# The opening stage of a hybrid encoder step: past gates summed earlier, a fourth modulation buffer, the first norm tile by tile

## The chip, the cores and the metric

One core of one Trainium2 chip runs the whole program. The metric is the device time of one execution in microseconds, as the median of several runs.

## The reference

One layer of a streaming encoder works on T = 1152 tokens: 1024 of one new stream (the prompt) and 8 x 16 of running streams (the samples), each of 1024 channels, all in float32.

```python
def rms_norm(x, g):
    inv = lax.rsqrt(jnp.mean(xf * xf, axis=-1, keepdims=True) + EPS)
    return (xf * inv).astype(x.dtype) * g

def ffn_sublayer(x, mod, base, g, w1, w3, w2):
    h = modulate(rms_norm(x, g), mod[:, base], mod[:, base + 1])   # h * (1 + scale) + shift
    gate = 1 + mod[:, base + 2][:, None, :]
    return x + MACARON_W * gate * swiglu(h, w1, w3, w2)
```

`mod` is silu(c) @ w_ada + b_ada, nine vectors of 1024 for each of the nine sequences. The layer is: this feed-forward, a mixer (a recurrent branch and a forgetting attention), a second feed-forward, and a final norm with a modulation of its own. The attention of the samples needs the running sum of `cache_logf`, the log forget gates of 1024 past positions for 8 streams and 16 heads (the **past gates**).

## The kernel before

**Layout.** Activations lie transposed: `x` is [128 channels, 8 channel tiles k, 1152 tokens], cut into three chunks c of 384 tokens (the third holds 256 of the prompt and all 128 of the samples). Every product is made of three passes (`mm3`, L299, L302, L303): an activation is split into a high part (`acts_hi`, by ScalarE) and the rest (`acts_lo`, by VectorE), a weight block of [128, 2048] into `w_hi` (ScalarE, L283) and `w_lo` (GpSimd, L289). A feed-forward goes over 11 pairs of 256 hidden channels; a pair is six `up` units (unit n is chunk n // 2, half n % 2, 48 matmuls each), then three `down` parts. In the first nine pairs of the first feed-forward a quarter of the rest of the modulation follows each of the first units (`ada_step`: TensorE makes a product, VectorE copies it to `mod_part`, TensorE turns it, VectorE adds the bias).

**Who sets the order.** Each engine runs a program written out by hand, and semaphores tie them; nothing is scheduled by a planner. What stands behind a waiting instruction on its engine waits too. All loads go through SyncE's queue in the order in which they are issued.

**The opening stage, by engine.** SyncE (`setup_sync`) loads the conditioning rows, the nine row tiles of x, small vectors, three slices of `w_ada` (slices 0 to 2, 2 MB each), the first two weight blocks, and, after the first slice was used (`ada_full`), slice 3 into the buffer of slice 0, the state rows, the forget columns `wfl_raw`, and the past gates, as eight loads whose pieces are 16 floats.
TensorE (`setup_tensor`) turns c and x, sums the squares for each chunk (`norm_sum_all`, L670, eight matmuls with a matrix of ones), and makes the first modulation: `product(h)` (L482) and `turn(h)` (L489) for four slices h, in the order product 0, product 1, turn 0, product 2, turn 1, turn 2, product 3, turn 3. Then `setup_rest_tensor` turns states and past gates (L551 to L558) and waits until both running sums are done (`past_summed` 3). Only then does `ffn_tensor` begin.
ScalarE (`setup_scalar`) squares x (L664), takes three roots (L676), makes three constants (L435 to L439), and goes on with `ffn_blocks_ahead` (the high parts of the first two weight blocks), the first norm, and `setup_rest_scalar` (an Exp and a Ln, each behind a table load, for the decay of the recurrence, and `wfl_hi`).
VectorE (`setup_vector`) moves x out of PSUM (L591), and for each chunk takes the reciprocal (L680) and multiplies the whole chunk by it (L685); then it copies the modulation rows (`copy_rows`, L601), adds biases (L565), and makes the scale (`final_scale`, L571, which releases the semaphore `mod_final`).

**The first norm.** Chunks 0 and 1 are made ahead of the feed-forward, chunk by chunk: VectorE modulates five of eight channel tiles (L707), ScalarE three (L718); ScalarE copies the chunk as a whole to `acts_hi` (L726), VectorE subtracts as a whole for `acts_lo` (L731) and releases `h_lo`, on which `up` waits. After chunk 1 VectorE runs `setup_rest_vector`: the rest of the decay (`log1p_vector`, `wfl_lo`), the states and the two running sums (L336). Chunk 2 is made behind unit 1. The later norms are made tile by tile with other helpers: `scale_tiles` (L815, x times scale times reciprocal, which is read in PSUM), `hi_tiles` (L844), `lo_tiles` (L860).

## Time and profile before

| | us |
|---|---|
| median of 3 runs | 3422.22 |
| lowest and highest | 3420.77, 3422.83 |
| the profiled execution | 3419.37 |
| its span in the trace | 3416.4 |

The profile is of one execution. Times in it run from the start of its span; the execution's own time is 2.97 us more than the span. A group of instructions is named by line, engine, operation and tile; "idle before" is the time in which its engine had nothing to do ahead of it, with what ended that time. PE is TensorE, PEld its weight loads, DVE VectorE, ACT ScalarE, POOL GpSimd, SP SyncE.

### The profile page before, as it was taken

How to read it: one execution, taken by the hardware profiler on the slowest of the kernel's cores; microseconds unless marked ns; L12 is line 12 of the kernel's file. 1: busy time of each engine (PE TensorE's matmuls, PEld its weight loads, DVE VectorE, ACT ScalarE, POOL GpSimd, SP SyncE). 2: the span in 40 equal slices, each digit the busy share in tenths (PEclk: the TensorE clock that was granted, in tenths of full speed). 3: DMA queues.
4: the chain of work that ended last, by engine and by line, in shares of the span. 5: the costliest groups of instructions: out<-in, count | busy, mean ns of one | idle time of the engine just before them, and what ended most of it. 6: DMA issues, size and time to landing. Idle time of an engine off the chain costs nothing.

```text
span 3416.4 us, 53101 instructions
## 1 busy us (share of the span) xinstructions
PE 3268.3 (96%) x20609; PEld 3113.7 (91%) x20609; DVE 1267.4 (37%) x2560; ACT 987.2 (29%) x1564; POOL 910.5 (27%) x471
## 2 busy tenths in 40 slices
PE   5999999999998999999999998889999999999997
PEld 3999999999988999998877797889989999999997
DVE  6322222222267342452222216775444222233225
ACT  3111111111143233333333416883232111111114
POOL 1222222222241211111110124773233222232223
PEclk7999999999999999999999999999999999999999
DMA  6322232231121321217777755664311111111101
GB/s 207 99 86 86 91 103 88 89 96 62 38 82 35 105 85 63 97 51 243 245 239 261 250 166 125 144 143 150 130 38 62 37 37 37 37 49 37 47 27 56
DMA packets 254331, 352.01 MB, mean 103 GB/s; under 512 B 40189, under 2 KB 190261, under 8 KB 253938
## 3 DMA queue, kind: packets, MB, share of 16 engines
q1 hardware_dynamic: 227762, 316.87, 29.4%
q10 hardware_dynamic: 26432, 33.18, 2.7%
q8 instruction: 103, 1.69, 0.2%
q14 instruction: 34, 0.28, 0.0%
HBM read 297.74 MB, written 48.07 MB: 101 GB/s over the span
## 4 chain that ended last, share of the span: by engine, by line
PE 87%; DVE 6%; issue 3%; ACT 3%; POOL 1%; DMA 0%; ACTq 0%; SPq 0%; DVEq 0%; POOLq 0%
PE psum L299 25%; PE psum L303 25%; PE psum L302 25%; PE psum L1779 2%; PE psum L2253 2%; PE psum L2272 1%; PE psum L482 1%; PE psum L1826 1%; DVE w_lo L2461 1%; PE psum L1420 1%; PE psum L1793 1%; PE psum L2238 1%; DVE acts_lo L860 1%; PE psum L489 1%; PE psum L2239 1%
## 5 line engine op out<-in xcount | busy, mean ns | idle before, releaser
L299 PE MATMUL psum<-acts_hi,w_hi 128*128 128x384 f32 x4032 | 1394.3, 346 | 26.8 <-DVE past_rows L336 25.2
L302 PE MATMUL psum<-acts_lo,w_hi 128*128 128x384 f32 x4032 | 1358.6, 337 | 6.0 <-issue 6.0
L303 PE MATMUL psum<-acts_hi,w_lo 128*128 128x384 f32 x4032 | 1358.8, 337 | 0.0
L299 PEld LDWEIGHTS psum<-acts_hi,w_hi 128*128 128x128 f32 x4032 | 761.5, 189 | 64.7 <-issue 47.5
L289 POOL TENSOR_TENSOR w_lo<-w_raw,w_hi 128x2048 fp32r<-128x2048 f32 x106 | 489.4, 4624 | 1175.1 <-ACT w_hi L283 1175.1
L303 PEld LDWEIGHTS psum<-acts_hi,w_lo 128*128 128x128 f32 x4032 | 760.7, 189 | 6.3 <-issue 6.3
L302 PEld LDWEIGHTS psum<-acts_lo,w_hi 128*128 128x128 f32 x4032 | 762.0, 189 | 4.4 <-issue 0.9
L1143 DVE TENSOR_TENSOR u_f<-psum,gated 128x384 f32<-128x384 f32 x132 | 73.6, 558 | 1020.2 <-ACT gated L1039 1020.2
L1094 POOL TENSOR_TENSOR u_lo<-u_f,u_hi 128x384 fp32r<-128x384 f32 x132 | 134.7, 1020 | 937.4 <-ACT u_hi L1044 937.4
L1214 DVE SCALAR_TENSOR_TENSOR x<-psum,mods,x 128x384 f32<-128x384 f32 (+1 forms) x552 | 314.5, 570 | 183.7 <-PE psum L303 183.7
L283 ACT ACTIVATE w_hi<-w_raw 128x2048 fp32r<-128x2048 f32 x106 | 200.4, 1909 | 572.0 <-PE psum L299 536.8
L299 PE MATMUL psum<-u_hi,w_hi 128*128 128x384 f32 x1056 | 356.4, 337 | 3.4 <-DVE x L1219 2.2
L303 PE MATMUL psum<-u_hi,w_lo 128*128 128x384 f32 x1056 | 355.6, 337 | 0.0
L302 PE MATMUL psum<-u_lo,w_hi 128*128 128x384 f32 x1056 | 355.5, 337 | 0.0
L1039 ACT ACTIVATE gated<-psum 128x384 f32<-128x384 f32 x132 | 64.8, 491 | 889.9 <-PE psum L303 889.8
L299 PEld LDWEIGHTS psum<-u_hi,w_hi 128*128 128x128 f32 x1056 | 199.0, 188 | 4.9 <-DVE x L1219 3.3
L302 PEld LDWEIGHTS psum<-u_lo,w_hi 128*128 128x128 f32 x1056 | 199.0, 188 | 0.3
L303 PEld LDWEIGHTS psum<-u_hi,w_lo 128*128 128x128 f32 x1056 | 199.1, 189 | 0.0
L1993 DVE COPY kTs<-psum 128x512 f32<-128x512 f32 x64 | 44.3, 692 | 249.8 <-PE psum L1779 249.8
L2253 PE MATMUL psum<-ident,pr 128*128 128x128 f32 x576 | 92.9, 285 | 31.9 <-DVE w_lo L2461 27.9
L2461 DVE TENSOR_TENSOR w_lo<-psum,w_hi 128x512 fp32r<-128x512 f32 (+1 forms) x192 | 100.4, 551 | 27.4 <-ACT w_hi L2338 26.7
L2253 PEld LDWEIGHTS psum<-ident,pr 128*128 128x128 f32 x576 | 63.4, 142 | 46.7 <-DVE w_lo L2461 29.9
(267 smaller groups left out, 2974.0 us busy)
## 6 DMA issues: line engine op xcount, KB each, us to landing
w_raw<-in_ffn_w SPq DMA_DIRECT2D x66, 1024.0 KB, 5.3
kc<-in_cache_k SPq DMA_DIRECT2D x32, 1024.0 KB, 6.7
vc<-in_cache_v SPq DMA_DIRECT2D x16, 2048.0 KB, 7.8
w_raw<-in_w_ada SPq DMA_DIRECT2D x28, 1024.0 KB, 5.0
w_raw<-in_w_in SPq DMA_DIRECT2D x28, 1024.0 KB, 5.3
sp<-sample_bias SPq DMA_DIRECT2D x128, 65.0 KB, 2.5
ada_w<-in_w_ada SPq DMA_DIRECT2D x4, 2048.0 KB, 15.1
w_raw<-in_w_ada_f SPq DMA_DIRECT2D x8, 1024.0 KB, 5.6
```

What stands on the lines that cost most here:

```text
L283: eng.activation(w_hi[st][:], w_raw[raw][:], ACT.Copy).then_inc(sem("w_hi_done"), 1)
L289: eng.tensor_tensor(w_lo[st][:], w_raw[raw][:], w_hi[st][:].bitcast(F32), ALU.subtract).then_inc(sem("w_lo_done"), 1)
L299: pass1 = eng.matmul(out, whi, ahi, start=first, stop=False)
L302: eng.matmul(out, whi, alo, start=False, stop=False)
L303: return eng.matmul(out, wlo, ahi, start=False, stop=last)
L1039: eng.activation(gated[n % 2][:], ps[2 * (n % 2)][:, 0:CH], ACT.Silu).then_inc(sem("gated_ready"), 1)
L1094: eng.tensor_tensor(u_lo[:, t, tokens_of(c)], u_f[n % 2][:], u_hi[:, t, tokens_of(c)].bitcast(F32), ALU.subtract).then_inc(sem("u_lo_done" ...
L1143: eng.tensor_tensor(u_f[n % 2][:], ps[2 * (n % 2) + 1][:, 0:CH], gated[n % 2][:], ALU.mult).then_inc(sem("u_free"), 1)
L1214: last = eng.scalar_tensor_tensor(xt[:, d, t0:t0 + cp], bank[:, 0:cp], mods[:, gate, d, 0:1], xt[:, d, t0:t0 + cp], ALU.mult, ALU.add)
L1779: last = eng.transpose(ps[TURNED][:, 128 * m:128 * m + 128], kc[:, 4 * half + m, 128 * p:128 * p + 128], ident[:])
L2253: last = eng.transpose(ps[bank_of(k, n)][:, 128 * (kb - k0):128 * (kb - k0) + 128], pr[k % 4][:, 128 * kb:128 * kb + 128], ident[:])
L2461: eng.tensor_tensor(pT_lo[q % 2][:, k0:k1, cols_], ps[bank_of(k, n)][:, 0:128 * (k1 - k0)].rearrange("p (k n) -> p k n", n=128), pT_hi[q % ...
```

## The change

The past gates and the states are loaded right behind x, the past gates in one load whose pieces are 128 floats, into `past_in`; GpSimd reorders them into `past_rows`; TensorE turns them between the sums of squares of chunk 0 and chunk 1 (half of the partitions at a time, with j, the position within a partition, as the innermost step of the result), and VectorE sums them (`past_sums`) behind the first reciprocal. `setup_rest_scalar` moves ahead of the first weight split, `setup_rest_vector` ahead of the first `copy_rows`. The fourth slice of `w_ada` gets `ada_w3`, over the rows of x, and is loaded ahead of the first weight blocks. `turn(1)` goes ahead of `product(2)`. The first norm uses the later norms' helpers; the whole multiply L685 goes, the samples' modulation moves to GpSimd, and the order on ScalarE is weight block 0, chunk 0, weight block 1, chunk 1. TensorE's first pair leaves the loop and is written out, and its first unit waits for weight block 1 only ahead of the second half of its products.

```diff
@@ -76,6 +76,9 @@
     xrowf = ExitStack()
     x_rows = [sb(xrowf, f"x_rows{n}", [128, D]) for n in range(T // 128)]
     xrowf.close()
+    adaf = ExitStack()
+    ada_w3 = sb(adaf, "ada_w3", [128, KT, 512])
+    adaf.close()
@@ -118,6 +121,7 @@
     adaf.close()
+    ada_w.append(ada_w3)
@@ -136,6 +140,7 @@
     past_rows = sb(setup, "past_rows", [128, PAST // 128, SB * H])
+    past_in = sb(setup, "past_in", [128, SB, PAST // 128, H])
@@ -378,21 +383,19 @@
-        def load_half(h, slot):
-            eng.dma_start(ada_w[slot][:], w_ada_v[:, :, 512 * h:512 * h + 512]).then_inc(sem(f"ada_loaded{slot}"), 16)
-        for h in range(3):
-            load_half(h, h)
-        ffn1_loads_ahead(eng)
-        eng.wait_ge(sem("ada_full"), 1)
-        load_half(3, 0)
+        eng.dma_start(past_in[:].rearrange("p b j h -> p b (j h)"),
+                      a["cache_logf"][0].rearrange("b (p j) h -> p b (j h)", p=128)).then_inc(sem("past_loaded"), 16)
         eng.dma_start(state_rows[0][:], a["state_rglru"].rearrange("l s (r c) -> (l s r) c", c=128)).then_inc(sem("state_loaded"), 16)
         conv_src = a["state_conv"].rearrange("l s j (r c) -> (l s j r) c", c=128)
         for n in range(2):
             eng.dma_start(state_rows[1 + n][:], conv_src[96 * n:96 * n + 96, :]).then_inc(sem("state_loaded"), 16)
-        eng.dma_start(wfl_raw[:], kview(a["w_in"][0])[:, :, COL_FL:COL_FL + H]).then_inc(sem("fl_loaded"), 16)
-        eng.dma_start(b_fgt_col[:], a["b_fgt"].rearrange("l h -> h l")).then_inc(sem("fl_loaded"), 16)
-        for b in range(SB):
-            eng.dma_start(past_rows[:, :, H * b:H * b + H], a["cache_logf"][0, b].rearrange("(k p) h -> p k h", p=128)).then_inc(sem("past_loaded"), 16)
+        for h in range(4):
+            if h == 3:
+                eng.wait_ge(sem("x_turned"), 2 * 4 + CREDIT)
+                eng.dma_start(wfl_raw[:], kview(a["w_in"][0])[:, :, COL_FL:COL_FL + H]).then_inc(sem("fl_loaded"), 16)
+                eng.dma_start(b_fgt_col[:], a["b_fgt"].rearrange("l h -> h l")).then_inc(sem("fl_loaded"), 16)
+            eng.dma_start(ada_w[h][:], w_ada_v[:, :, 512 * h:512 * h + 512]).then_inc(sem(f"ada_loaded{h}"), 16)
+        ffn1_loads_ahead(eng)
@@ -437,6 +440,7 @@
         eng.activation(pick_r[:], mask_f[0:ST, :], ACT.Copy).then_inc(sem("const_split"), 1)
+        setup_rest_scalar(eng)
@@ -468,6 +472,9 @@
                           pattern=[[-1, 128]], channel_multiplier=1).then_inc(sem("const"), 1)
+        eng.wait_ge(sem("past_loaded"), 16)
+        eng.tensor_copy(past_rows[:].rearrange("p j (b h) -> p j b h", b=SB),
+                        past_in[:].rearrange("p b j h -> p j b h")).then_inc(sem("past_loaded"), 1)
         eng.wait_ge(sem("const_split"), 2)
@@ -490,7 +497,7 @@
-    START_BANKS = (5, 3)
+    START_BANKS = (7, 3)
@@ -519,14 +526,17 @@
         eng.wait_ge(sem("params_ready"), 1)
-        for c in range(NC):
-            norm_sum_all(eng, 0, c)
+        eng.wait_ge(sem("x_moved"), 2 * (T // 128) + CREDIT)
+        norm_sum_all(eng, 0, 0)
+        setup_rest_tensor(eng)
+        norm_sum_all(eng, 0, 1)
+        norm_sum_all(eng, 0, 2)
 
         def product(h):
-            eng.wait_ge(sem(f"ada_loaded{h % 3}"), 16 * (h // 3 + 1))
+            eng.wait_ge(sem(f"ada_loaded{h}"), 16)
             if h >= 2:
                 eng.wait_ge(sem("mod_rows_ready"), h - 1)
-            ada_product(eng, ps[START_BANKS[h % 2]], ada_w[h % 3], 512)
+            ada_product(eng, ps[START_BANKS[h % 2]], ada_w[h], 512)
 
         def turn(h):
...
         eng.wait_ge(sem("c_act"), 2)
-        eng.wait_ge(sem("x_moved"), 2 * (T // 128) + CREDIT)
+        eng.wait_ge(sem("past_summed"), 1)
         product(0)
         product(1)
         turn(0)
+        turn(1)
         product(2)
-        turn(1)
         turn(2)
         product(3)
         turn(3)
@@ -548,16 +558,17 @@
     def setup_rest_tensor(eng):
 
         eng.wait_ge(sem("state_loaded"), 48)
-        eng.transpose(ps[0][:, 0:64], state_rows[0][:], ident[0:64, 0:64])
+        eng.transpose(ps[7][:, 0:64], state_rows[0][:], ident[0:64, 0:64])
         for n in range(2):
-            last = eng.transpose(ps[0][:, 64 + 96 * n:160 + 96 * n], state_rows[1 + n][:], ident[0:96, 0:96])
+            last = eng.transpose(ps[7][:, 64 + 96 * n:160 + 96 * n], state_rows[1 + n][:], ident[0:96, 0:96])
         last.then_inc(sem("states_turned"), 1)
-        eng.wait_ge(sem("past_loaded"), 16 * SB)
+        eng.wait_ge(sem("past_loaded"), 17)
         for half in range(2):
-            for k in range(4):
-                last = eng.transpose(ps[1 + half][:, 128 * k:128 * k + 128], past_rows[:, 4 * half + k, :], ident[:])
+            rows = slice(64 * half, 64 * half + 64)
+            for j in range(PAST // 128):
+                last = eng.transpose(ps[1 + half].rearrange("q (p j) -> q p j", j=PAST // 128)[:, :, j],
+                                     past_rows[rows, j, :], ident[rows, rows])
             last.then_inc(sem("states_turned"), 1)
-        eng.wait_ge(sem("past_summed"), 3)
@@ -590,9 +601,11 @@
-        for c in range(NC):
-            norm_inverse(eng, 0, c)
-            norm_times_inverse(eng, 0, c)
+        norm_inverse(eng, 0, 0)
+        past_sums(eng)
+        norm_inverse(eng, 0, 1)
+        norm_inverse(eng, 0, 2)
+        setup_rest_vector(eng)
@@ -624,18 +637,20 @@
         eng.tensor_tensor(wfl_lo[:], wfl_raw[:], wfl_hi[:].bitcast(F32), ALU.subtract).then_inc(sem("past_summed"), 1)
+        eng.memset(tiny_col[:], 2.0 ** -100)
+
+    def past_sums(eng):
         eng.wait_ge(sem("states_turned"), 1)
-        eng.tensor_copy(h0[:], ps[0][:, 0:64])
-        eng.tensor_copy(conv_state[:], ps[0][:, 64:256])
+        eng.tensor_copy(h0[:], ps[7][:, 0:64])
+        eng.tensor_copy(conv_state[:], ps[7][:, 64:256])
         past_f = past_rows[:].rearrange("p k n -> p (k n)")
         for half in range(2):
             eng.wait_ge(sem("states_turned"), 3)
             if half:
-                eng.wait_ge(sem("past_summed"), 2)
+                eng.wait_ge(sem("past_summed"), 1)
             running_sums(eng, past_f[:, 512 * half:512 * half + 512], ps[1 + half], past_f[:, 511:512] if half else 0.0).then_inc(sem("past_summed"), 1)
-        eng.wait_ge(sem("past_summed"), 3)
+        eng.wait_ge(sem("past_summed"), 2)
         eng.tensor_copy(past_last[:], past_rows[:, PAST // 128 - 1, 127:128])
...
 
-    STAT_BANKS = [(6, 7, 4), (7, 2, 5), (6, 7, 6), (7, 2, 7)]
+    STAT_BANKS = [(0, 5, 6), (7, 2, 5), (6, 7, 6), (7, 2, 7)]
@@ -679,67 +694,22 @@
-    def norm_times_inverse(eng, n, c):
-
...
-    def norm_scale(eng, n, c):
-
...
-    def norm_hi(eng, n, c):
-
...
-    def norm_lo(eng, n, c):
-
...
     def norm_scalar(eng):
-        for c in range(2):
-            norm_hi(eng, 0, c)
+        eng.wait_ge(sem("ada_full"), FIRST - 1)
+        ffn_split_hi(eng, 0, 0, 0)
+        hi_tiles(eng, 0, 0)
+        ffn_split_hi(eng, 0, 0, 1)
+        hi_tiles(eng, 0, 1)
 
     def norm_vector(eng):
-        for c in range(2):
-            norm_scale(eng, 0, c)
-            norm_lo(eng, 0, c)
+        scale_tiles(eng, 0, 0)
+        lo_tiles(eng, 0, 0)
+        scale_tiles(eng, 0, 1)
+        lo_tiles(eng, 0, 1)
+        samples_inverse(eng, 0)
@@ -756,13 +726,13 @@
     def normed_count(n, c, k):
-        return NC + (n - 1) * NC * KT + c * KT + k + 1
+        return n * NC * KT + c * KT + k + 1
 
     def tile_count(n, c, k):
-        return NC + (n - 1) * (NC * KT + 1) + c * KT + k + 1
+        return n * (NC * KT + 1) + c * KT + k + 1
 
     def sample_count(n, step):
-        return 1 + 3 * (n - 1) + step
+        return 3 * n + step
@@ -954,9 +924,11 @@
             if n == 0:
-                wait_block(eng, block0 + i * 3 + 1)
+                wait_block(eng, block0 + i * 3 + (0 if first and f == 0 else 1))
             for which, bank in ((0, 2 * (n % 2)), (1, 2 * (n % 2) + 1)):
                 whi, wlo = wcols(FFN_SLOTS[which][2], t)
+                if first and f == 0 and (n, which) == (0, 1):
+                    wait_block(eng, block0 + i * 3 + 1)
                 for k in range(KT):
@@ -1011,11 +983,10 @@
+        body(0, first=True, ada=f == 0)
         if f == 0:
-            with eng.Fori(0, ADA_PAIRS) as i:
+            with eng.Fori(1, ADA_PAIRS) as i:
                 body(i, ada=True)
-        else:
-            body(0, first=True)
@@ -1043,7 +1014,8 @@
             if f == 0 and first_step and n == 1:
-                norm_hi(eng, 0, 2)
+                hi_tiles(eng, 0, 2)
+                hi_samples(eng, 0)
@@ -1108,6 +1080,7 @@
         if f == 0:
             for j in range(2):
                 split_lo(eng, block0 + j, FFN_SLOTS[j])
+            samples_modulate(eng, 0)
         with eng.Fori(0, FF_PAIRS - 1) as i:
@@ -1154,9 +1127,10 @@
             for n in range(6):
                 unit(i, n)
+                if f == 0 and first_step and n == 0:
+                    scale_tiles(eng, 0, 2)
                 if f == 0 and first_step and n == 1:
-                    norm_scale(eng, 0, 2)
-                    norm_lo(eng, 0, 2)
+                    lo_tiles(eng, 0, 2)
@@ -1361,7 +1335,7 @@
     def proj_tensor(eng):
-        eng.wait_ge(sem("past_summed"), 1)
+        eng.wait_ge(sem("past_summed"), 3)
...
@@ -2694,12 +2668,6 @@
-    def ffn_blocks_ahead(eng):
-        eng.wait_ge(sem("ada_full"), 3)
-        ffn_split_hi(eng, 0, 0, 0)
-        eng.wait_ge(sem("ada_full"), FIRST)
-        ffn_split_hi(eng, 0, 0, 1)
@@ -2717,9 +2685,7 @@
         setup_scalar(eng)
-        ffn_blocks_ahead(eng)
         norm_scalar(eng)
-        setup_rest_scalar(eng)
         ffn_scalar(eng, 0)
@@ -2746,7 +2712,6 @@
         setup_tensor(eng)
-        setup_rest_tensor(eng)
         ffn_tensor(eng, 0)
@@ -2760,7 +2725,6 @@
         setup_vector(eng)
         norm_vector(eng)
-        setup_rest_vector(eng)
         ffn_vector(eng, 0)
```

## Rows read from the trace of the kernel before

**Rows 1.** The page, busy time of TensorE over the span: us (share), instructions.

```profile
PE 3268.3 (96%) x20609; PEld 3113.7 (91%) x20609; DVE 1267.4 (37%) x2560; ACT 987.2 (29%) x1564; POOL 910.5 (27%) x471
```

**Rows 2.** Waits of TensorE, whole span: us in total, times, longest us.

```profile
PE psum L299 <- DVE past_rows L336: 25.2, 1, 25.2
...
PE psum L302 <- issue: 6.0, 2, 3.0
```

**Rows 3.** Timeline of TensorE, opening: start us, us, instructions, [idle before <-releaser].

```profile
19.70 15.65 PE L670 MATMUL psum<-sq,ones 128*128 128x384 f32 x48
...
44.45 1.88 PE L489 MATMUL psum<-cols,mod_rows 128*128 128x9 f32 x8 [5.54 <-DVE mod_rows L601]
46.26 3.64 PE L482 MATMUL psum<-ada_w,states 128*32 128x512 f32 x16
...
56.72 1.25 PE L558 MATMUL psum<-ident,past_rows 128*128 128x128 f32 x8
83.20 0.68 PE L299 MATMUL psum<-acts_hi,w_hi 128*128 128x384 f32 x1 [25.23 <-DVE past_rows L336]
```

**Rows 4.** Timeline of VectorE, opening; L591 moves x, L571 makes the scale.

```profile
15.35 6.06 DVE L591 COPY x<-psum 128x512 f32<-128x512 f32 x10
...
40.44 3.35 DVE L685 TENSOR_TENSOR h_f<-x,psum 128x3072 f32<-128x3072 f32 x1
43.71 1.28 DVE L601 COPY mod_rows<-psum 128x512 f32<-128x512 f32 x2
...
56.63 4.51 DVE L571 SCALAR_TENSOR_TENSOR mods<-mods,params 128x72 f32<-128x72 f32 x1
...
78.51 0.12 DVE L363 TENSOR_TENSOR lam_t<-lam_t 128x8 f32<-128x8 f32 x1
...
79.55 0.28 DVE L626 TENSOR_TENSOR wfl_lo<-wfl_raw,wfl_hi 128x128 fp32r<-128x128 f32 x1
...
80.15 1.21 DVE L336 TENSOR_TENSOR_SCAN past_rows<-ones,psum 128x512 f32<-128x512 f32 x1
...
104.15 0.56 DVE L1143 TENSOR_TENSOR u_f<-psum,gated 128x384 f32<-128x384 f32 x1 [8.59 <-ACT gated L1039]
...
129.66 0.56 DVE L1143 TENSOR_TENSOR u_f<-psum,gated 128x384 f32<-128x384 f32 x1 [10.13 <-ACT gated L1039]
...
139.56 0.56 DVE L1143 TENSOR_TENSOR u_f<-psum,gated 128x384 f32<-128x384 f32 x1 [8.62 <-ACT gated L1039]
```

**Rows 5.** Timeline of ScalarE, opening.

```profile
35.38 0.56 ACT L676 ACTIVATE psum<-psum,cols 128x384 f32<-128x384 f32 x1 [4.61 <-PE psum L670]
...
37.12 0.31 ACT L439 ACTIVATE pick_r<-mask_f 16x128 fp32r<-16x128 f32 x1 [0.76 <-POOL mask_f L474]
...
74.17 0.19 ACT L444 ACTIVATE lam_t<-params 128x8 f32<-128x8 f32 x1
...
75.90 1.28 ACT L346 ACT_TABLE_LOAD   x1
```

**Rows 6.** Timeline of GpSimd, opening: the first two weight blocks' low parts.

```profile
51.96 9.09 POOL L289 TENSOR_TENSOR w_lo<-w_raw,w_hi 128x2048 fp32r<-128x2048 f32 x2 [14.87 <-ACT w_hi L283]
```

**Rows 7.** Timeline of VectorE, later norms, 945 to 1010 us.

```profile
987.43 4.31 DVE L860 SCALAR_TENSOR_TENSOR acts_lo<-h_f,mods,acts_hi 128x384 fp32r<-128x384 f32 x8
```

**Rows 8.** Timeline of VectorE, 2490 to 2585 us.

```profile
2549.45 4.29 DVE L815 SCALAR_TENSOR_TENSOR h_f<-x,mods,psum 128x384 f32<-128x384 f32 x8
```

**Rows 9.** Timeline of GpSimd, 2490 to 2585 us.

```profile
2571.47 4.80 POOL L289 TENSOR_TENSOR w_lo<-w_raw,w_hi 128x2048 fp32r<-128x2048 f32 x1
```

**Rows 10.** Instructions of line L860: ns min/median/max, first and last start us, forms.

```profile
L860 DVE SCALAR_TENSOR_TENSOR acts_lo<-h_f,mods,acts_hi x48: 472/606/4834, 957.0 to 2579.2; 128x384 fp32r<-128x384 f32 x32, 128x256 fp32r<-128x256 f32 x16
```

**Rows 11.** Stage table: stretch, us, busy us (x) by engine, clock, DMA share, GB/s.

```profile
83.20:88.10 4.90, 4.90 (x15) 4.90 (x16) 0.00 (x0) 3.19 (x2) 2.13 (x1) 0.50 0.95 313
```

**Rows 12.** Timeline of SyncE's queue: start us, us to issue, transfers.

```profile
37.26 0.37 SPq L382 DMA_DIRECT2D ada_w<-in_w_ada  x1
```

**Rows 13.** DMA, loads issued 37.6 to 38.2 us: count, KB each, us to landing.

```profile
h_rows<-in_state_rglru SPq DMA_DIRECT2D x1, 32.0 KB, 7.8
```

More of the change, by code:

```diff
@@ L633, in setup_rest_vector @@
             if half:
-                eng.wait_ge(sem("past_summed"), 2)
+                eng.wait_ge(sem("past_summed"), 1)
             running_sums(eng, past_f[:, 512 * half:512 * half + 512], ps[1 + half], past_f[:, 511:512] if half else 0.0).then_inc(sem("past_summed"), 1)
-        eng.wait_ge(sem("past_summed"), 3)
+        eng.wait_ge(sem("past_summed"), 2)
         eng.tensor_copy(past_last[:], past_rows[:, PAST // 128 - 1, 127:128])
-        eng.memset(tiny_col[:], 2.0 ** -100)
     def mods_rest(eng):
@@ L680, in norm_inverse @@
         eng.reciprocal(stats(n, c), stats(n, c)).then_inc(sem("inv_ready"), 1)
-    def norm_times_inverse(eng, n, c):
-        eng.wait_ge(sem("inv_ready"), NC * n + c + 1)
-        eng.tensor_tensor(h_f[:, :, tokens_of(c)], x[:, :, tokens_of(c)],
-                          stats(n, c).unsqueeze(1).to_broadcast([128, KT, CH]), ALU.mult).then_inc(sem("x_normed"), 1)
     def mods_ready(eng, n):
         eng.wait_ge(sem("mod_final"), 1 if n == 0 else 7)
-    def norm_scale(eng, n, c):
-        g = NC * n + c
-        shift, scale = NORM_MODS[n]
-        if n > 0:
-            norm_times_inverse(eng, n, c)
-        mods_ready(eng, n)
-        eng.wait_ge(sem("x_normed"), g + 1)
-        cp = CH if c < NC - 1 else CP
-        if c == NC - 1:
-            hs = h_f[:, :, TP:T].rearrange("p k (s t) -> p k s t", s=SB)
-            eng.tensor_tensor(hs, hs, seq_bc(scale), ALU.mult).then_inc(sem("mod_step"), 1)
-            eng.wait_ge(sem("mod_step"), n + 1)
-            eng.tensor_tensor(hs, hs, seq_bc(shift), ALU.add)
-        for k in range(K_ON_ACT):
-            hp = h_f[:, k, CH * c:CH * c + cp]
-            last = eng.tensor_scalar(hp, hp, mods[:, scale, k, 0:1], mods[:, shift, k, 0:1], ALU.mult, ALU.add)
-        last.then_inc(sem("h_ready"), 1)
@@ L710, in norm_modulate @@
-    def norm_modulate(eng, n, c):
-        cp = CH if c < NC - 1 else CP
-        shift, scale = NORM_MODS[n]
-        mods_ready(eng, n)
-        eng.wait_ge(sem("x_normed"), NC * n + c + 1)
-        for k in range(K_ON_ACT, KT):
-            hp = h_f[:, k, CH * c:CH * c + cp]
-            last = eng.activation(hp, hp, ACT.Identity, scale=mods[:, scale, k, 0:1], bias=mods[:, shift, k, 0:1])
-        last.then_inc(sem("h_modulated"), 1)
-    def norm_hi(eng, n, c):
-        norm_modulate(eng, n, c)
-        eng.wait_ge(sem("h_modulated"), NC * n + c + 1)
-        eng.wait_ge(sem("h_ready"), NC * n + c + 1)
-        eng.activation(acts_hi[:, :, tokens_of(c)], h_f[:, :, tokens_of(c)], ACT.Copy).then_inc(sem("h_hi"), 1)
@@ L728, in norm_lo @@
-    def norm_lo(eng, n, c):
-        eng.wait_ge(sem("h_hi"), NC * n + c + 1)
-        eng.tensor_tensor(acts_lo[:, :, tokens_of(c)], h_f[:, :, tokens_of(c)],
-                          acts_hi[:, :, tokens_of(c)].bitcast(F32), ALU.subtract).then_inc(sem("h_lo"), 1)
-    def norm_scalar(eng):
-        for c in range(2):
-            norm_hi(eng, 0, c)
-    def norm_vector(eng):
-        for c in range(2):
-            norm_scale(eng, 0, c)
-            norm_lo(eng, 0, c)
+    def norm_scalar(eng):
+        eng.wait_ge(sem("ada_full"), FIRST - 1)
[3 more added lines that the diff above has]
+        hi_tiles(eng, 0, 1)
@@ L1245, in turn @@
             else:
-                eng.wait_ge(sem("h_modulated"), NC + c * KT + KT)
+                eng.wait_ge(sem("h_modulated"), c * KT + KT)
             if tile == 1:
```

## The prediction

> **What bounds the kernel now.** The page comes first: TensorE is busy for 96% of the span [rows 1], so time can come back only where it stands still. The list of its waits then names the places. One wait of 25.2 us stands out: the first product of the feed-forward waits for the running sums of the past gates [rows 2]. Its timeline shows the same as a start: TensorE is done with the opening at about 58.0 us (56.72 + 1.25) and begins the feed-forward at 83.20 [rows 3]. The timelines of the other engines, read between those two points, show what was done meanwhile: the scale on VectorE ends at 61.14 (56.63 + 4.51), then chunks 0 and 1 of the norm are made, and only behind both come the sums [rows 4]. A second loss lies inside the first pair: unit 1 is taken up by VectorE at 104.15, unit 3 at 129.66, which is 25.51 us for two units, while units 3 and 4 stand 9.90 us apart [rows 4]. Two units at 9.90 would be 19.80, so 5.7 us are lost there, behind the third chunk's norm. After this pair TensorE runs nearly without waits, so what the opening gains or loses reaches the end whole.
>
> **Part 1: the way to the first copy of modulation rows.** The first sum of squares now waits for all of x, which is there at 21.4 us (15.35 + 6.06), not 19.70: 1.7 us later. The three sums took 15.65 together, 5.22 each [rows 3]. Behind the first stand the turns. The state rows are the old ones, some 0.6 us; the eight turns of past gates took 1.25 us [rows 3] and become sixteen of half the rows. That costs 1.25 us if the columns count and 2.5 if each instruction does; I take 1.9, between them. The third sum then ends at 21.5 + 15.65 + 0.6 + 1.9 = 39.6 us, where the third root started at 35.38 before [rows 5]: 4.3 later. The loads and GpSimd's reordering lie beside this: GpSimd took 9.09 us for two passes over 128x2048 with two inputs [rows 6], so at most 2.3 us for 1024 with one, and the turns need it only at 26.7 us (21.5 + 5.2). If that cover is gone, the wait stands on TensorE (third rival).
>
> ScalarE then does its constants, which end 2.05 us behind the root's start (37.12 + 0.31 - 35.38), and the decay moved here: from 74.17 to 77.18 (75.90 + 1.28), plus one small Ln of about 0.2, is 3.2 us [rows 5]. So the Ln is done at 39.6 + 2.05 + 3.2 = 44.9. VectorE's part behind it ran from 78.51 to 79.83, 1.3 us [rows 4]; its earlier steps lie beside the table load. With 0.1 to hand over, the first copy of rows starts at 46.3 instead of 43.71 [rows 4], **2.6 us later**. The whole multiplies L685 that go (3.35 us each) were what held it at 43.71 [rows 4]; the running sums take their place on VectorE, but while TensorE makes the second sum, so they cost nothing.
>
> **Part 2: from the copy to the scale.** This took 12.92 us (43.71 to 56.63) [rows 4]. The pieces stay; with turn 1 ahead of product 2 the third copy (0.64) and a bias (about 0.2) are no longer beside a turn, so I add 0.8; the ends are 0 and, if TensorE's clock rises earlier and product 2 takes half of its 3.64 us [rows 3], -1.8. That puts the scale at 60.0. It will not run at once. Of the 72 elements it works on, an instruction should take a fraction of a microsecond, yet it lasted 4.51 us and ended at 61.14, just as GpSimd ended its two weight passes, 61.05 (51.96 + 9.09) [rows 4, 6]. So it stood behind GpSimd. In the changed kernel only weight block 0 is split there. GpSimd began 2.06 us after product 2 ended (49.90, 46.26 + 3.64) [rows 3, 6], and product 2 now ends at about 54.6 at the latest (46.3, 0.74 to the turn, two turns of 1.88, 3.64, and 0.2), or 1.8 earlier: the pass of 4.55 us then ends between 59.4 and 61.2. The scale is done at about **61.0, where it was before**; the fourth slice in its own buffer is there long before it is needed, as slice 3 was before, and brings nothing by itself.
>
> **Part 3: from the scale to the first product.** Before: 83.20 - 61.14 = 22.06 us for two chunks, the decay and the sums. Now one chunk by tiles: eight scale tiles took 4.29 us [rows 8] and eight low tiles 4.31 [rows 7] where the later norms run, the high tiles beside them. Handing over is about 0.2. That alone would start TensorE at 61.0 + 8.8 = 69.8.
>
> But the second weight block's split now stands behind chunk 0's high tiles on ScalarE. The last of those ends about 0.6 us (a tile) behind the scale tiles, at 65.9; GpSimd starts 2.06 us later, at 68.0, as above. The low tiles began at 65.3, so five of eight are done (0.54 each) and three are not. One low tile in the trace took 4.834 us against a median of 0.606 [rows 10], where GpSimd made a weight pass of 4.80 us [rows 9]: 4.2 us lost. Scale tiles read the reciprocal in PSUM and have no such outlier that I found, low tiles have both inputs in SBUF. I charge **4.2 us**, with ends 0 and 4.6: the first product at 74.0, 9.2 us earlier than before.
>
> The Trainium skill, Advanced Engine Details and Errata, section VectorE Performance Modes, says that GpSimd and those VectorE instructions that use two ports, the doubled modes, block each other. By that note alone a low tile, float32 with two inputs, would not be held, and the first product would come at 69.8. The skill's SBUF — State Buffer, section SBUF: two separate sides, adds VectorE instructions with two SBUF inputs, and the row of 4.834 us sides with it.
>
> TensorE starts at the lower clock either way: the first 4.9 us behind the old wait ran at a granted clock of 0.50, which is 1.2 of its 2.4 GHz [rows 11], and it stands idle ahead of the first product here too. No change.
>
> **Part 4: the third chunk.** Its scale tiles now follow unit 0 on VectorE, its low tiles unit 1, the samples' modulation is on GpSimd, long done. VectorE takes unit 1 at about 95.0 (104.15 - 9.2), and TensorE needs the next modulation copy behind unit 2, about 9 us later (the spacing of 9.90 less its step), at 104; eight shorter tiles, beside ScalarE's, take at most 4.3, the samples' parts some 2.5, so it is there at about 102. The wait goes: **5.7 us**. The margin is 2 us.
>
> **Part 5: edits with one answer.** Writing out TensorE's first pair issues the same instructions; the second feed-forward is already written so. Unknown is its loading of code: 0 to 6.0 us (the two stops "issue" of 3.0 us each [rows 2] are the nearest); I take 0, as no such stop lies in either feed-forward. The finer wait for weight block 1 costs nothing: it is there at 72.6, before the first product. Semaphore counts and PSUM banks change no work.
>
> **Sum.** -9.2 - 5.7 = -14.9 us. The profiled execution took 3419.37 (span 3416.4 and 2.97 around it), so 3404.5 by its own time; it lies 2.85 us under the median, which gives **3407.3** against 3422.22, or -0.44%. This kernel's measurement can tell about 0.2%, 6.8 us, from no change.
>
> **Rivals.** *No collision on the low tiles.* If GpSimd starts 1.6 us later than I say, or a low tile is not held, by the first of the two rules above, 4.2 us come back: 3403.1. For it: three tiles are a thin margin. Against it: the row of 4.834 us. Chance 0.15.
>
> *A wait takes the old one's place in the first pair.* If VectorE, with twice as many tile instructions to hand to and fro with ScalarE and with GpSimd's low parts of unit 1 in between, gets to the modulation copy after TensorE, the loss of the first pair returns, up to 5.7: 3413.0. It decides from 2 us of delay on. Chance 0.13.
>
> *Slower: the past gates come late.* TensorE's second and third sums now stand behind them. A state load of 32 KB issued behind a slice of 2 MB, itself issued at 37.26 [rows 12], took 7.8 us to land [rows 13], so landing about 45.5. If the early loads shared the queue with all that follows instead of going first, they would land when the queue runs empty, at about 47.5 (45.5 and the past gates' own share), GpSimd would be done at 49.7, and the turns would come 23.0 us behind 26.7: 3430.3. The time is slower by over 0.2% from 21.7 us of that wait on. Against it: that same row shows a queue served in order, and the past gates are issued ahead of the slices. Chance 0.05.
>
> *Smaller gains together*, the wait in the pair and stops for code, 3419 at the most: chance 0.07, within 0.2% of before.
>
> **Chances and range.** My forecast has 0.60, 3404.5 to 3410.5 by the bounds on turns, clock and code. With the first two rivals 0.88 lies within 3402.5 and 3413.5, the range. Faster by over 0.2%: 0.60 + 0.15 + 0.13 = 0.88; same 0.07; slower 0.05.
>
> **What would show it.** Right: the first product at 74 us; one low tile of chunk 0 lasting 4 to 5 us beside GpSimd's second weight pass; the scale done at 61; units 1 to 4 taken up 9.5 to 9.9 us apart. Wrong: a wait of TensorE on the past gates' reordering at 27 us; the first copy of rows later than 48; a low tile series of 4.3 us; a clock of 0.50 in unit 3.

## The result and the profile after

| | before | after |
|---|---|---|
| median, us (lowest to highest, runs) | 3422.52 (3420.77 to 3424.86, 4) | **3399.73** (3396.57 to 3401.43, 4) |
| profiled execution, us (span) | 3419.37 (3416.4) | 3401.43 (3399.6) |

The ratio is 0.9937, with a 95% interval of 0.9925 to 0.9948: faster by 22.8 us, where 14.9 were predicted, and 2.8 us below the range. The two profiled executions differ by less, 16.8 us of span, since that of before lies under its median and that of after over it. All lines of time below are set against these two.

The timeline of TensorE after the change answers to [rows 3]. Some line numbers have moved: L685 sums squares, L489 makes products, L496 and L569 turn, L304 is the first pass of a product.

```profile
21.97 5.40 PE L685 MATMUL psum<-sq,ones 128*128 128x384 f32 x16 [1.64 <-issue]
...
27.81 1.02 PE L569 MATMUL psum<-ident,past_rows 64*128 64x64 f32 x16
28.76 10.59 PE L685 MATMUL psum<-sq,ones 128*128 128x384 f32 x32
...
46.65 1.06 PE L496 MATMUL psum<-cols,mod_rows 128*128 128x9 f32 x8 [3.73 <-DVE mod_rows L614]
48.09 1.85 PE L496 MATMUL psum<-cols,mod_rows 128*128 128x9 f32 x8 [0.38 <-DVE mods L576]
49.87 3.64 PE L489 MATMUL psum<-ada_w,states 128*32 128x512 f32 x16
54.51 1.85 PE L496 MATMUL psum<-cols,mod_rows 128*128 128x9 f32 x8 [1.01 <-DVE mods L576]
56.29 3.64 PE L489 MATMUL psum<-ada_w,states 128*32 128x512 f32 x16
60.75 1.87 PE L496 MATMUL psum<-cols,mod_rows 128*128 128x9 f32 x8 [0.81 <-DVE mod_rows L614]
71.78 0.66 PE L304 MATMUL psum<-acts_hi,w_hi 128*128 128x384 f32 x1 [9.16 <-issue]
...
98.30 1.93 PE L489 MATMUL psum<-w_raw,states 128*32 128x256 f32 x16 [6.57 <-DMA w_raw<-in_w_ada]
```

The feed-forward begins at 71.78 us instead of 83.20, 11.4 earlier. The last row is new: in the first pair TensorE waits 6.57 us for a transfer, the second quarter of the next modulation weights. VectorE's timeline (compare [rows 4]; L614 copies rows, L582 makes the scale, L785 the scale tiles, L830 the low tiles, L795 the samples):

```profile
45.91 0.69 DVE L614 COPY mod_rows<-psum 128x512 f32<-128x512 f32 x1
...
62.89 0.23 DVE L582 SCALAR_TENSOR_TENSOR mods<-mods,params 128x72 f32<-128x72 f32 x1
63.16 4.29 DVE L785 SCALAR_TENSOR_TENSOR h_f<-x,mods,psum 128x384 f32<-128x384 f32 x8
67.36 4.32 DVE L830 SCALAR_TENSOR_TENSOR acts_lo<-h_f,mods,acts_hi 128x384 fp32r<-128x384 f32 x8
71.60 4.29 DVE L785 SCALAR_TENSOR_TENSOR h_f<-x,mods,psum 128x384 f32<-128x384 f32 x8
...
80.19 1.21 DVE L795 TENSOR_TENSOR h_f<-x,psum 128x1024 f32<-128x1024 f32 x1
```

GpSimd's timeline (compare [rows 6]; L294 makes the low part of a weight block, L804 and L806 modulate the samples):

```profile
55.57 4.54 POOL L294 TENSOR_TENSOR w_lo<-w_raw,w_hi 128x2048 fp32r<-128x2048 f32 x1 [14.47 <-ACT w_hi L288]
69.98 6.17 POOL L294 TENSOR_TENSOR w_lo<-w_raw,w_hi 128x2048 fp32r<-128x2048 f32 x1 [9.87 <-ACT w_hi L288]
81.55 1.94 POOL L804 TENSOR_TENSOR h_f<-h_f,mods 128x1024 f32<-128x1024 f32 x1 [5.40 <-DVE h_f L795]
83.57 1.95 POOL L806 TENSOR_TENSOR h_f<-h_f,mods 128x1024 f32<-128x1024 f32 x1
85.47 4.62 POOL L294 TENSOR_TENSOR w_lo<-w_raw,w_hi 128x2048 fp32r<-128x2048 f32 x1
```

And SyncE's queue between 75 and 100 us:

```profile
90.11 0.37 SPq L280 DMA_DIRECT2D w_raw<-in_ffn_w  x1
90.52 0.58 SPq L865 DMA_DIRECT2D w_raw<-in_w_ada  x1
```

Read together, the last three views show the new wait as a chain: VectorE's sample step (80.19), GpSimd's two sample steps, only then its pass over weight block 2 (ends at 90.09), and with that the buffer is free for the next weight block (90.11), behind which the modulation quarter is issued (90.52). ScalarE had the high part of block 2 ready at 78.35, so GpSimd came to its pass 7.1 us late:

```profile
76.44 1.91 ACT L288 ACTIVATE w_hi<-w_raw 128x2048 fp32r<-128x2048 f32 x1
```

Unit 2 is taken up by VectorE at 110.34, 18.4 us behind unit 1 (91.94). At the end of the first pair (its last unit at 138.99 instead of 148.41) 9.4 us are left of the 11.4.

Matching TensorE's instructions of both traces gives the rest. The lead is 9.8 us at 974 us, and still 9.8 within the first pass of the mixer's projection loop (a product at 1250.09 before stands at 1240.32 after). It is 22.4 within the third pass (1450.09 against 1427.67), and 18.5 at the last product (3411.91 against 3393.38). So **12.6 us appeared in the mixer, in a loop that the change doesn't touch**: from the one product to the other TensorE took 200.0 us before and 187.4 after. Below, the way between these two products is called the mixer's stretch. There the trace of before has its two stops "issue" of 3.0 us [rows 2], one soon behind each jump back to the loop's head, and right at the jump a shorter pause, which the list puts down to ScalarE:

```profile
PE psum L1431 <- ACT st L1488: 2.3, 2, 1.1
```

The trace of after has no wait of TensorE between 1240 and 1450 us. The four pauses add up to 8.3 us. Most of the rest lies in the products behind each stop, which ran at the lower clock (1.2 of 2.4 GHz) before it came back; stretch, us, busy us (x) by engine, clock, DMA share, GB/s:

```profile
1288.00:1293.00 5.00, 4.57 (x15) 4.57 (x15) 0.00 (x0) 0.00 (x0) 0.00 (x0) 0.50 0.03 10
1293.00:1300.00 7.00, 7.00 (x44) 6.93 (x43) 0.00 (x0) 1.77 (x4) 0.00 (x0) 1.00 0.10 28
```

The stops come with transfers of the instruction queue. DMA queues between 1240 and 1450 us, packets, MB, share, first of before:

```profile
q8 instruction: 14, 0.23, 0.4%
```

and of after:

```profile
q8 instruction: 2, 0.03, 0.1%
```

Before, the loop's code is fetched anew in each of the two passes in this stretch, 7 packets each; after, it stays.

### The profile page after: what moved, and what is told of

The parts are those of the page before. It is cut to its first block, busy times and chain, and to the rows that moved or that the text cites. A ratio compares the mean times of both kernels' runs of the same rounds, so it can differ in the third digit from the quotient of the medians.

```text
span 3399.6 us, 53111 instructions
## 1 busy us (share of the span) xinstructions
PE 3269.5 (96%) x20617; PEld 3113.2 (92%) x20617; DVE 1260.7 (37%) x2587; ACT 986.6 (29%) x1577; POOL 916.5 (27%) x474
## 4 chain that ended last, share of the span: by engine, by line
PE 86%; DVE 5%; issue 3%; ACT 3%; SPq 1%; DMA 1%; POOL 1%; ACTq 0%; DVEq 0%; POOLq 0%
PE psum L304 25%; PE psum L308 25%; PE psum L307 25%; PE psum L1753 2%; PE psum L2227 1%; PE psum L489 1%; PE psum L2246 1%; PE psum L1800 1%; DVE w_lo L2435 1%; PE psum L1394 1%; PE psum L1767 1%; DVE acts_lo L830 1%; DVE h_f L785 1%; PE psum L496 1%; PE psum L2212 1%
## 5 line engine op out<-in xcount | busy, mean ns | idle before, releaser
L304 PE MATMUL psum<-acts_hi,w_hi 128*128 128x384 f32 x4032 | 1392.9, 345 | 10.8 <-issue 9.2
L304 PEld LDWEIGHTS psum<-acts_hi,w_hi 128*128 128x128 f32 x4032 | 760.4, 189 | 48.4 <-issue 31.2
L294 POOL TENSOR_TENSOR w_lo<-w_raw,w_hi 128x2048 fp32r<-128x2048 f32 x106 | 491.0, 4639 | 1148.1 <-ACT w_hi L288 1148.1
L304 PE MATMUL psum<-u_hi,w_hi 128*128 128x384 f32 x1056 | 356.3, 337 | 3.4 <-DVE x L1193 2.2
L304 PEld LDWEIGHTS psum<-u_hi,w_hi 128*128 128x128 f32 x1056 | 199.0, 188 | 4.9 <-DVE x L1193 3.3
```

The source lines that it names most:

```text
L294: eng.tensor_tensor(w_lo[st][:], w_raw[raw][:], w_hi[st][:].bitcast(F32), ALU.subtract).then_inc(sem("w_lo_done"), 1)
L304: pass1 = eng.matmul(out, whi, ahi, start=first, stop=False)
```

## The experiments

Each ratio is to the kernel before on the same chip (median 3421.49 us for the four runs whose names begin with e, 3420.28 for f1, f2, g and h, 3420.70 for f3 and both i).

### Undoing the written-out pair, and doing it alone

`e1_rolled` is the changed kernel with TensorE's first pair back in its loop, where the finer wait for weight block 1 then stands in every pair; `e2_writtenout` is the kernel before with only that pair written out. Of the first, the loop:

```diff
...
-        body(0, first=True, ada=f == 0)
         if f == 0:
-            with eng.Fori(1, ADA_PAIRS) as i:
+            with eng.Fori(0, ADA_PAIRS) as i:
                 body(i, ada=True)
+        else:
+            body(0, first=True)
```

> The changed kernel, but TensorE's first pair is back in the loop of nine pairs (the finer wait on weight block 1 is kept, in every pair). Theory (code): writing the pair out moved TensorE's later code, and by that the mixer's projection loop stopped being loaded anew in each pass; back in the loop, two stops 'issue' of 3.0 us with a low clock behind them return near 1280 and 1420 us, the instruction queue moves some 103 packets instead of 90, and the time is about 12 us over the changed kernel's 3399.7, at 3412. The opening and the first pair stay as they are (first product at 71.8). Rival: the mixer gained because everything came earlier and the loads fell otherwise; then the time stays at 3399.7 within 2 us, without stops.

Measured: 3414.69 us, ratio 0.9982 (0.9972 to 0.9991). The opening is that of the changed kernel (first product at 72.50), and the stops are back, longer than before: each now holds the whole pause at its jump. The mixer's stretch takes 202.2 us. Waits of TensorE:

```profile
PE psum L1406 <- issue: 11.0, 2, 5.6
```

> The kernel before, with one edit alone: TensorE's first pair of the first feed-forward is written out ahead of a loop of eight. Theory (code): the two stops in the mixer go although nothing else is changed, about -12.4 us: 3410, first product still at 83.2. Rival: the stops are not of the code's place: 3422.5 as before, with the stops.

Measured: 3422.82 us, ratio 1.0005 (0.9995 to 1.0014), 14 packets, two stops, the longer 3.9 us, and 201.9 us for the stretch. My theory that writing out the pair removes the stops fell: it takes the pair and the other edits together. What they alter in common for the projection loop is how many instructions of TensorE stand ahead of it. Hence the next theory: the loop's *place*.

### The place alone

`f1_before_shifted` and `f3_before_17` are the kernel before with 45 and 17 more instructions at the head of TensorE's program; `f2_after_shifted` is the changed kernel with 200. They are waits for something that is already there (two waits make one instruction).

```diff
         eng.sem_inc(sem("pa_s"), 16)
+        for _ in range(90):
+            eng.wait_ge(sem("w_used"), 1)
         eng.wait_ge(sem("const"), CONSTS)
```

> The kernel before, with 45 more instructions at the head of TensorE's program (waits on a semaphore that already stands, in the first 4 us in which TensorE idles); nothing else differs, and no arithmetic is added. Theory (the place of the mixer's projection loop in TensorE's code decides whether it is fetched again in every pass): with the code ahead of it 45 instructions longer the loop stays loaded; the two stops without a semaphore in the mixer go, the instruction queue moves 1 or 2 packets between 1240 and 1450 instead of 14, and the median is about 14 us lower, 3408 (3404 to 3413). Rival (the stops went because of something else that the change does in the opening): 14 packets, both stops, 3422.

Measured: **3408.35 us**, ratio 0.9965 (0.9952 to 0.9977), 2 packets, no stop in the mixer. The first product stands at 83.47, as before. So 11.9 us of the median came from 45 instructions that do nothing. The mixer's stretch takes 187.4 us, as in the changed kernel: 12.6 gained. To the end 3.9 of that go again, in steps near 1750, 2550 and 3385 us, and the changed kernel loses 3.9 behind the mixer too; what takes them was not tested.

> The kernel before with 17 more instructions at the head of TensorE's program. By the place theory the projection loop is still fetched in every pass (it stays loaded only from about 25 more on), and its first instructions lie closer to the end of their fetched piece than before, as in the run with the rolled pair: stops of about 5 us instead of 3.0 at the two jumps back, 14 or 15 packets, median 3422 to 3427. If the length of the stops has nothing to do with the place: stops of 3.0.

Measured: 3424.67 us, ratio 1.0009 (1.0000 to 1.0019), 14 packets, and both stops longer, as expected; they hold the whole pause at the jump, which before was 1.1 + 3.0. Waits of TensorE:

```profile
PE psum L1433 <- issue: 10.7, 2, 5.4
```

> The changed kernel, with 200 more instructions at the head of TensorE's program (the same kind of wait, in stretches in which TensorE idles for loads). Theory of the place: the loop lies badly again; the stops return, 14 packets between 1240 and 1450, about 15 us more, 3414 (3410 to 3420), and the opening up to the first product within 1 us of the changed kernel's 71.8. Rival: no stops, 3400, or only what the waits themselves cost in the opening.

Measured: 3415.62 us, ratio 0.9982 (0.9973 to 0.9992): the number expected, but not its reason. Waits of TensorE:

```profile
PE psum L513 <- issue: 14.3, 1, 14.3
...
PE psum L307 <- issue: 0.9, 2, 0.5
```

The 200 instructions cost 12 us in the opening (first product at 83.72), which I had taken for nothing. The loop is indeed fetched again (15 packets), but the stops are 0.5 us each, behind pauses of up to 1.2 at the jump, and the mixer's stretch takes 191.5 us, 4.1 more than in the changed kernel. So a fetch need not cost as much.

The stops at this jump had 0.5, 3.0, 3.9, 5.4 and 5.6 us, and the traces show one pattern in them. In all ten jumps with a fetch (before, `e1`, `e2`, `f2`, `f3`) TensorE is past its stop 5.7 to 6.0 us behind the last product of the pass. What differs is how many products and turns it makes in that time: none in `f3` and `e1`, 2 in `e2`, 7 in the kernel before, 22 in `f2`. The 17 instructions of `f3` moved the stop from behind 7 products and turns, each with its weight load, to the loop's head. This fits code that arrives piece by piece, with an edge between two pieces that the place sets; where the edges lie was not measured. The data traffic doesn't tell the cases apart: over the 6 us behind the jump the mean DMA share was 0.64 before, 0.61 in `f2`, 0.52 in `f3` and 0.60 in `f1`, which didn't stop.

### The new wait in the first pair

`e3_unit1_early`: SyncE issues the second modulation quarter ahead of the weight block whose buffer is late.

```diff
             unit(i, 0, view[:, :, ds(col, 256)])
+            if first:
+                unit(i, 1, view[:, :, ds(col + 256, 256)])
             ffn_load(eng, 0, i + 1, 0)
-            for u in range(1, 4):
+            for u in range(2 if first else 1, 4):
```

> The changed kernel, but SyncE issues the second quarter of the modulation's weights in the first pair ahead of the first weight block of the next pair. Theory: the 6.6 us wait of TensorE behind unit 1 is a load that stood in SyncE's queue behind a wait on GpSimd's third weight pass (90.1 us); issued at about 83 it lands at 88, units 1 and 2 are taken up 9.9 us apart instead of 18.4, and the time falls by about 8.5 us to 3391. Rival: VectorE's copy or the samples' part is late as well, then another wait stands in the same place: a gain under 3 us, 3397 or more.

Measured: 3389.98 us, ratio 0.9909 (0.9892 to 0.9925). The wait is gone; timeline of TensorE:

```profile
92.40 1.07 PE L489 MATMUL psum<-w_raw,states 128*32 128x256 f32 x16
...
102.30 1.07 PE L489 MATMUL psum<-w_raw,states 128*32 128x256 f32 x16
```

The modulation products behind units 0 to 2 now stand 9.9 us apart (the first at 82.52). The end of the chain read above is shown by this: the transfer was late by its place in SyncE's queue, not by the traffic. That the samples' steps are what holds the block ahead of it is read from the views; no run moved them.

### The order of the turns

`e4_turn_order`: product 2 ahead of turn 1 again, as before.

```diff
         turn(0)
+        product(2)
         turn(1)
-        product(2)
         turn(2)
```

> The changed kernel, with product 2 ahead of turn 1 again, as before the change. Theory: the new order leaves TensorE standing about 1 us behind each step, its clock stays at 0.50 through products 2 and 3 and turns 1 to 3, and the way from the first copy of rows to the scale takes 17.0 us instead of 12.9; with the old order product 3 takes 1.9 us again instead of 3.6, the scale is made about 4 us earlier (58.7), and the time falls by about 4 us to 3395.7. Rival: the order is free or better as changed, since the clock stays low in either case: 3399.7 to 3401.

Measured: 3394.37 us, ratio 0.9925 (0.9909 to 0.9942), first product at 67.55. The interval overlaps that of the change, and part of the 4.2 us by which this first product leads 71.78 is TensorE's clock. That shows in executions of one order at two clocks. `e2_writtenout`, with the old order, has the opening of the kernel before, and its timeline of TensorE reads:

```profile
44.37 1.87 PE L489 MATMUL psum<-cols,mod_rows 128*128 128x9 f32 x8 [5.53 <-DVE mod_rows L601]
...
58.24 1.88 PE L489 MATMUL psum<-cols,mod_rows 128*128 128x9 f32 x8 [0.81 <-DVE mod_rows L601]
```

From the first to the end of the last turn this is 15.75 us. In the profiled execution of before the same instructions took 11.92 (44.45 to 56.37). From 51.6 on a turn took 1.03 to 1.06 us and a product 1.92, not 1.85 and 3.64: the granted clock was 1.00 from 51.6 to 56.4 us, and 0.50 in `e2_writtenout` from 51.6 to 60.1 (2.4 and 1.2 GHz). `e4_turn_order` itself took 12.05 us (46.34 to 58.39), with the clock up for a part. The new order took 16.78 us at the low clock in `e3_unit1_early` (46.33 to 63.11), and 13.11 in `h_split_early` below (46.34 to 59.45), where the clock rose. So the new order costs 1.0 to 1.2 us, and the moment at which the clock rises is worth 3.7 to 3.8 in either order. What sets that moment stays open: `i_after_again` and three others of the new order stayed at the low clock from 48 us to the last turn, three had it rise between 53 and 70 us; in two of these the edit takes effect only later.

> The changed kernel once more, beside the others of this job: median 3397 to 3402; the second modulation quarter again about 6.5 us late in the first pair. If the opening's clock comes up at another moment of the opening in each execution, the first product lies anywhere from 68 to 73 us in its profile; if the new order of the turns fixes it, at 71.8 within 0.5.

Measured: 3397.82 us, ratio 0.9934 (0.9916 to 0.9952), first product at 71.68, the quarter late by 6.6 us.

`g_both` is `e3_unit1_early` and `e4_turn_order` together.

> The changed kernel with both single edits together: SyncE issues the second modulation quarter ahead of the next weight block in the first pair, and TensorE computes product 2 ahead of turn 1 again. If the two stalls are independent the gains add: 3399.7 - 9.7 - 5.3 = 3384.7 (3382 to 3388). Rival (the opening's gain is taken back by a wait for the same transfers in the first pair): 3390.

Measured: **3387.55 us**, ratio 0.9901 (0.9882 to 0.9920), the lowest median of all: first product at 68.69, units 9.9 us apart. It lies in the range, 2.9 us short of the sum that I gave. Set against `e3_unit1_early` it is 2.4 us lower, within both intervals; the order's own 1.0 to 1.2 would fit as well.

### Who waits, GpSimd or VectorE

`h_split_early` splits weight block 1 on ScalarE ahead of chunk 0's high tiles; `i_split_mid` does it behind the first of them (the diff is of this one).

```diff
-        hi_tiles(eng, 0, 0)
+        hi_tile(eng, 0, 0, 0)
         ffn_split_hi(eng, 0, 0, 1)
+        for k in range(1, KT):
+            hi_tile(eng, 0, 0, k)
```

> The changed kernel, but ScalarE splits weight block 1 ahead of chunk 0's high tiles, so that GpSimd's pass over block 1 (4.6 to 6.2 us) falls beside VectorE's scale tiles or low tiles of chunk 0 instead of behind them. Theory of my prediction (a long GpSimd pass holds a VectorE operation with two SBUF inputs for its whole length): one VectorE tile of 3 to 5 us in the trace, the first product 3 to 4 us later than 71.8, the median 3402 to 3404. Rival (in a row of VectorE operations without a gap GpSimd is the one that waits, as its 6.17 us pass at 69.98 seems to show): all low tiles of chunk 0 stay near 0.53 us, the first product stays within 1 us of 71.8, the median 3398 to 3401.

Measured: 3403.54 us, ratio 0.9950 (0.9932 to 0.9968). This told nothing of the low tiles: GpSimd's second pass ran beside the scale tiles, which took their usual 4.29 us, and ended at 64.78, as the low tiles began at 64.61. That the median lies where the theory put it is no support: the trace has no long tile, its first product stands at 69.03, and it is that of the fastest of the four executions (3396.90). What makes the others 6 to 8 us longer stays open.

> The changed kernel, but ScalarE splits weight block 1 right behind chunk 0's first high tile, so that GpSimd's pass over it starts about 66.3, while VectorE still writes the scale tiles, and is under way when the low tiles begin at 67.4. Theory (whoever begins first keeps the other waiting: a pass of GpSimd that is under way holds a VectorE operation with two SBUF inputs to its end; a closed row of such VectorE operations holds GpSimd): the first low tile takes 3.5 to 4 us instead of 0.53, the first product comes 3.4 us later, at 75 to 76, and the median 3 us above the changed kernel of the same job. Rival (low tiles are not held by GpSimd in this place, whatever begins first): all low tiles near 0.53 us, first product 71 to 73, no difference.

Measured: 3400.18 us, ratio 0.9944 (0.9926 to 0.9963), 2.4 above `i_after_again`, within both intervals. In the trace the collision happens. GpSimd, then VectorE (the series that took 4.32):

```profile
63.65 4.52 POOL L294 TENSOR_TENSOR w_lo<-w_raw,w_hi 128x2048 fp32r<-128x2048 f32 x1 [3.33 <-ACT w_hi L288]
...
64.65 7.63 DVE L832 SCALAR_TENSOR_TENSOR acts_lo<-h_f,mods,acts_hi 128x384 fp32r<-128x384 f32 x8
```

The same line by duration, ns min/median/max:

```profile
L832 DVE SCALAR_TENSOR_TENSOR acts_lo<-h_f,mods,acts_hi x8: 607/609/3928, 64.7 to 71.7; 128x384 fp32r<-128x384 f32 x8
```

One tile took 3.93 us, from its start to the end of GpSimd's pass and a tile more. The first product came at 72.39, 3.4 us behind the 69.03 of `h_split_early`, whose clock rose alike.

## Why the prediction was wrong, step by step

By the profiled executions the terms are: first product -11.4 us (predicted -9.2), first pair +2.0 (predicted -5.7), mixer and what follows it -12.6 + 3.9 = -8.7 (predicted 0). With 0.4 us gained between pair and mixer and 1.7 lost behind the last product that is -16.8, the difference of the spans. Two misses of 7.7 and 8.7 us with opposite signs nearly cancel, so that the forecast came as near as it did is luck. The medians differ by 6.0 us more: the profiled execution of before lies 3.15 us under its median, that of after 1.70 over, and 1.1 lies outside the spans.

**Part 5 failed, "I take 0, as no such stop lies in either feed-forward."** It asked whether the written-out pair would bring stops of its own where it stands. The runs show that added instructions move the code behind them, and that the mixer's loop was the one to gain: 12.6 us in the change and in `f1_before_shifted` alike, 3.9 given back later in both. The row that carried my bound of 6.0 us [rows 2] was the thing itself. I read it as a price, and did not ask what two stops without a semaphore, at the jump of one loop, come from. My bounds also had the wrong sign: code could only cost. The Trainium skill, Advanced Engine Details and Errata, section ISA Cache, gives TensorE 128 KB for instructions in lines of 16 KB, 256 instructions. An estimate from that page: the loop's pass has 780 products and turns and 65 other instructions in the trace; with a weight load for each of the 780, as the page of the profile counts them, that is 1625, or 6.35 lines, which lie across seven or eight lines by place, out of eight. The 7 packets a pass, of 16 KB each (0.23 MB in 14), agree; that eight lines are what fails is not shown.

**Part 4 failed, "the samples' modulation is on GpSimd, long done".** The old wait went, but the samples' steps stand ahead of weight block 2 in GpSimd's program, and SyncE's queue waits for that block. I followed VectorE to the modulation copy and did not follow the moved step on the engine that received it, with what is queued behind it there. `e3_unit1_early` removes the new wait of 6.6 us. My second rival had the right place and the wrong engine: it asked for a delay on VectorE.

**Part 3, the charge of 4.2 us, did not fall due.** The eight low tiles took 4.32 us, none over 0.62 in chunk 0. GpSimd was the one that waited: its pass over weight block 1 was ready at about 70 and took 6.17 us instead of 4.54, about 1.6 more, until the row of low tiles ended at 71.6. `i_split_mid` shows the mechanism to be right once GpSimd comes first: 3.93 us for a tile, 3.4 on the first product. The Trainium skill, SBUF — State Buffer, section SBUF: two separate sides, says that whichever starts first keeps the other out; I had used half of that sentence. The trace agrees with it there. But the page speaks of one instruction, and GpSimd waited for three of 0.53 us, until VectorE turned to tiles that read PSUM. That is not so everywhere. In the trace of before a GpSimd step that came up in a row of low tiles went ahead of the third of them, and the row took 5.06 us instead of 4.31:

```profile
2554.44 5.06 DVE L860 SCALAR_TENSOR_TENSOR acts_lo<-h_f,mods,acts_hi 128x384 fp32r<-128x384 f32 x8
```

```profile
2555.16 1.28 POOL L789 TENSOR_TENSOR z<-z 128x384 f32<-128x384 f32 x1 [7.76 <-ACT z L781]
```

The pass behind my 4.834 [rows 9] also started, at 2571.47, in a row of low tiles that had begun at 2570.91. What lets GpSimd in at one place and not at the other stays open. (The tile of 4.834 us is one of 128x256, which takes 0.47 otherwise, so it lost 4.4, not 4.2.)

**Part 2 was mis-sized in its base.** The term added for the new order, 0.8 us, measures 1.0 to 1.2. But 12.92 us from the copy to the scale came from one execution with an early rise of the clock; now it took 17.0 (45.91 to 62.89). Before, the late case was half hidden, since the scale stood behind GpSimd until 61.05 anyway [rows 6]: the first product of `e2_writtenout` came at 85.75, 2.6 later than in the profile of before, with the end of the last turn 3.8 later. The scale is done at 63.1 instead of the 61.0 predicted. With the charge that did not fall due, 2.1 - 4.2, this is nearly the 2.2 us by which the first product beat its 74.0. That the scale stands behind GpSimd was read rightly: in `i_split_mid` it took 0.64 us instead of 0.23 and ended at 60.41, as the pass ended at 60.32.

**Part 1 was right.** The first copy of rows began at 45.91 (predicted 46.3), and TensorE did not wait for the past gates at all, against the third rival. The sixteen turns took 1.02 us, below the lower bound of 1.25 that I had from eight of twice the rows.

## What to carry to other kernels

A stop of TensorE that waits for no semaphore, at the jump of a loop, belongs beside the instruction queue's packets in that stretch: if they repeat with each pass, the loop does not stay loaded, and any edit ahead of it, even idle instructions, can give or take time there (12.6 us here), so test the edit and the shift apart. Count the whole stretch: the listed stops were 6.0 us of it. For a step moved to another engine, follow that engine's program to the next step that frees a buffer, and the load queue behind it. A duration taken from one execution at a changing clock needs a second one, or both ends in the range.

## What was not expected of the hardware

- The stop at one jump grew from 3.0 to 5.4 us with 17 instructions of shift and vanished with 45, while a place with the loop fetched in each pass had stops of only 0.5. In each case with a fetch TensorE was past the stop 5.7 to 6.0 us behind the pass's last product.
- Two hundred instructions that only wait, each on a semaphore that already stood, cost 12 us up to the first product (14.7 up to the first turn of modulation rows, at 61.31 instead of 46.65); the 80 of them between the turns of c (15.34) and those of x (23.28) took 7.94 us, 0.1 us each.
- A row of VectorE tiles with both inputs in SBUF kept GpSimd's pass out for 1.6 us, three tiles long, while elsewhere a GpSimd step went ahead within such a row; a pass that was under way kept one such tile for 3.3.
